# The first feature chunk behind a full-width norm taken as two products in a hybrid decoder trunk

## The reference, cut to what matters

```python
for layer in range(DEPTH):
    h = rms_norm(r, norm_mix_pre[layer])
    proj = h @ w_in[layer]
    ...                                   # two attention branches, gates
    mix = (...) @ w_out[layer]
    r = r + rms_norm(mix, norm_mix_post[layer])
    h = rms_norm(r, norm_ffn_pre[layer])
    gu = h @ w_gate_up[layer]
    ff = (silu(gu[..., :D_FF]) * gu[..., D_FF:]) @ w_down[layer]
    r = r + rms_norm(ff, norm_ffn_post[layer])
```

## Time and profile before

| | us |
|---|---|
| median of 3 runs (lowest to highest) | 797.07 (796.63 to 797.28) |
| the profiled execution's own time | 796.88 |
| its span | 795.1 |
| PE busy (share of the span) | 787.6 (99%) |
| PEld busy | 763.7 (96%) |
| DVE busy | 575.2 (72%) |
| ACT busy | 452.1 (57%) |
| POOL busy | 135.8 (17%) |

### The profile page before, as it was taken

The page is one execution under the profiler, slowest core; times in us unless marked ns, Lnnn a source line. Parts: engine busy times, 40 slices in busy tenths (PEclk is TensorE's granted clock), DMA queues, the critical chain, the costliest instruction groups (busy, mean ns, idle before and its releaser), DMA issues.

```text
span 795.1 us, 16819 instructions
## 1 busy us (share of the span) xinstructions
PE 787.6 (99%) x6300; PEld 763.7 (96%) x6300; DVE 575.2 (72%) x964; ACT 452.1 (57%) x766; POOL 135.8 (17%) x146
## 2 busy tenths in 40 slices
PE   9999999999999999999999999999999999999997
PEld 9999899999999999999999999999999999999885
DVE  6899787686787666766668987976867977676432
ACT  6657665674565444455557467566755754544331
POOL 0212000233421111101122202000433211111000
PEclk9999999999999999999999999999999999999999
DMA  9767333355266555355654674334652766657951
GB/s 335 260 219 240 129 108 105 108 182 162 57 202 216 165 169 174 119 165 169 195 174 134 197 239 149 107 106 133 181 168 77 220 212 183 193 175 197 274 134 53
DMA packets 55531, 134.87 MB, mean 170 GB/s; under 512 B 20896, under 2 KB 21536, under 8 KB 55344
## 3 DMA queue, kind: packets, MB, share of 16 engines
q1 hardware_dynamic: 38608, 131.43, 52.5%
q10 hardware_dynamic: 16864, 2.62, 1.9%
HBM read 131.93 MB, written 2.10 MB: 169 GB/s over the span
## 4 chain that ended last, share of the span: by engine, by line
PE 98%; DMA 0%; DVE 0%; ACT 0%; issue 0%; DVEq 0%
PE bank L1327 25%; PE bank L1329 24%; PE bank L1328 24%; PE bank L1361 4%; PE bank L1748 3%; PE bank L1749 3%; PE bank L1747 3%; PE bank L1352 2%; PE bank L1602 2%; PE bank L1571 2%; PE bank L1621 1%; PE bank L1420 1%; PE bank L1573 1%; PE bank L1377 1%; PE bank L1576 1%; PE bank L1381 1%
## 5 line engine op out<-in xcount | busy, mean ns | idle before, releaser
L880 DVE TENSOR_TENSOR w_lo<-w_raw,w_hi 128x1024 fp32r<-128x1024 f32 x246 | 331.0, 1348 | 37.7 <-ACT w_hi L436 34.3
L1327 PE MATMUL bank<-h_hi,w_hi 128*128 128x272 f32 (+1 forms) x1200 | 346.0, 288 | 0.0
L1329 PE MATMUL bank<-h_hi,w_lo 128*128 128x272 f32 (+1 forms) x1200 | 342.8, 286 | 0.0
L1328 PE MATMUL bank<-h_lo,w_hi 128*128 128x272 f32 (+1 forms) x1200 | 341.9, 285 | 0.0
L436 ACT ACTIVATE w_hi<-w_raw 128x1024 fp32r<-128x1024 f32 x246 | 258.9, 1056 | 121.5 <-PE bank L1329 56.4
L1327 PEld LDWEIGHTS bank<-h_hi,w_hi 128*128 128x128 f32 x1200 | 226.2, 189 | 0.5
L1329 PEld LDWEIGHTS bank<-h_hi,w_lo 128*128 128x128 f32 x1200 | 226.2, 189 | 0.0
L1328 PEld LDWEIGHTS bank<-h_lo,w_hi 128*128 128x128 f32 x1200 | 226.0, 188 | 0.0
L845 POOL TENSOR_TENSOR pbuf<-sbuf,ubuf 128x272 f32<-128x272 f32 (+1 forms) x44 | 38.4, 874 | 205.6 <-DVE ubuf L1257 204.0
L778 POOL TENSOR_TENSOR acc<-acc,sq 128x272 f32<-128x272 f32 (+1 forms) x45 | 47.5, 1055 | 137.0 <-ACT sq L449 136.8
L1257 DVE TENSOR_TENSOR ubuf<-bank,rstd_h 128x272 f32<-128x272 f32 (+1 forms) x44 | 18.9, 431 | 44.8 <-PE bank L1329 44.8
(11 more groups left out here) (238 smaller groups left out, 1234.7 us busy)
## 6 DMA issues: line engine op xcount, KB each, us to landing
w_raw<-weights SPq DMA_DIRECT2D x216, 512.0 KB, 4.0
w_raw<-weights SPq DMA_DIRECT2D x16, 384.0 KB, 3.6
w_raw<-weights SPq DMA_DIRECT2D x16, 320.0 KB, 2.9
w_first<-first_weights SPq DMA_DIRECT2D x2, 512.0 KB, 7.6
x_tok<-x_rows SPq DMA_DIRECT2D x1, 1024.0 KB, 11.3
turn<-y ACTq DMA_DIRECT2D x4, 256.0 KB, 7.2
r_tok<-turn ACTq DMA_DIRECT2D x8, 128.0 KB, 5.6
out_tokens<-o_tok SPq DMA_DIRECT2D x4, 256.0 KB, 2.0
```

What stands on the lines that cost most here:

```text
L880: dve.tensor_tensor(w_lo[:, n % RING, :], w_raw[:, n % RAW, :], w_hi[:, n % RING, :].bitcast(f32), ALU.subtract).then_inc(lo_ready, 1)
L1327: pe.matmul(dst, wh, hi, start=first, stop=False)
L1328: pe.matmul(dst, wh, lo, start=False, stop=False)
L1329: return pe.matmul(dst, wl, hi, start=False, stop=last)
```

## The change

What TensorE needs of chunk 0 is the high and low part of (old residual + normed part) times the gain. Since the product is linear, it is now taken in two: one on the old residual's chunk 0, which is known long before, and one on the normed part alone. Three matmuls per tile on the old residual's parts (`old_hi`, `old_lo`) are issued ahead of and behind the spread, where dummies stood (two tiles each; 8 dummies are left, ahead of `first_tiles`). `first_tiles` then takes the normed part (`new_hi`, `new_lo`) in place of chunk 0. ScalarE makes `old_hi` after squaring tile 5 of the projection, VectorE `old_lo` after copying tile 6. VectorE's add of chunk 0 to the residual moves from the head of `residual` behind the fourth chunk's add, since the full chunk 0 is still needed (`hh[0]`, `hl[0]`, by later tiles, and its square). Chunks are made in the order 1, 2, 3, 4, 0, 5, 6, 7.

```diff
+CHUNK_ORDER = [1, 2, 3, 4, 0, 5, 6, 7]
...
+        (old_hi, old_lo, new_hi, new_lo, new), _end = place(att0 + 4 * 2 * FC * TOK, [
+            ("old_hi", [P, TOK], f32r), ("old_lo", [P, TOK], f32r), ("new_hi", [P, TOK], f32r), ("new_lo", [P, TOK], f32r), ("new", [P, TOK], f32)])
...
 # ScalarE
+            def old_high(b):
+                t0 = boundary_from(b)
+                act.activation(old_hi[:, t0:], r[:, 0, t0:], ACT.Copy, scale=first_gain(b)).then_inc(old_hi_ready, 1)
...
             def boundary(b, K, g, l):
-                for c in range(KC):
-                    act.wait_ge(r_ready, KC * (b - 1) + c + 1)
+                def high(c):
                     act.activation(hh[:, c, t0:], r[:, c, t0:], ACT.Copy, scale=gain[:, l, g + c:g + c + 1]).then_inc(h_hi, 1)
-                    square(K, c, r[:, c, t0:], t0)
+                act.wait_ge(new_ready, b)
+                act.activation(new_hi[:, t0:], new[:, t0:], ACT.Copy, scale=first_gain(b)).then_inc(new_hi_ready, 1)
+                for c in CHUNK_ORDER:
+                    if c == 0:
+                        act.wait_ge(r_first_ready, b)
+                    else:
+                        act.wait_ge(r_ready, (KC - 1) * (b - 1) + c)
+                    high(c)
+                    square(K, CHUNK_ORDER.index(c), r[:, c, t0:], t0)
...
                     square_tile(K0 + POST_MIX, TL("out") + m, m)
+                    if m == 5:
+                        old_high(2 * l + 1)
 # VectorE
+                dve.scalar_tensor_tensor(out=new[:, t0:], in0=y[:, 0, t0:], scalar=gain[:, lp, gp:gp + 1],
+                                         in1=ps[7][:, 64 + t0:64 + TOK], op0=ALU.mult, op1=ALU.mult).then_inc(new_ready, 1)
...
-                product(0)
-                add(0)
                 product(1)
                 add(1)
-                for c in range(2, KC):
+                product(2)
+                new_low()
+                add(2)
+                for c in range(3, KC):
                     product(c)
                     lo_part(b, c - 2, *nxt(b), t0)
                     add(c)
+                    if c == 4:
+                        dve.wait_ge(new_ready, b)
+                        dve.tensor_tensor(r[:, 0, t0:], r[:, 0, t0:], new[:, t0:], ALU.add).then_inc(r_first_ready, 1)
+                    if c == 6:
+                        lo_part(b, 0, *nxt(b), t0)
...
                     to_y(K0 + POST_MIX, TL("out") + m, m)
+                    if m == 6:
+                        old_low(2 * l + 1)
 # TensorE
+            def old_part(b, tiles):
+                pe.wait_ge(old_lo_ready, b)
+                slot_ready(tiles[-1][1])
+                for t, n, _, t0 in tiles:
+                    bank_free(t)
+                    dst = ps[bank_of(t)][:, t0:TOK]
+                    pe.matmul(dst, w_hi[:, n % RING, 0:P], old_hi[:, t0:], start=True, stop=False)
+                    pe.matmul(dst, w_lo[:, n % RING, 0:P], old_hi[:, t0:], start=False, stop=False)
+                    pe.matmul(dst, w_hi[:, n % RING, 0:P], old_lo[:, t0:], start=False, stop=False)
...
-            def post_norm(K):
+            def post_norm(K, b, tiles):
                 norm_sums(K, 7, t0)
-                keep_clock(10)
+                old_part(b, tiles[:2])
                 norm_spread(K, 7, t0)
-                keep_clock(28)
+                old_part(b, tiles[2:])
+                keep_clock(8)
```

More of the change, by code:

```diff
@@ L900, in lo_part @@
             def lo_part(b, c, g, l, t0):
-                dve.wait_ge(h_hi, KC * b + c + 1)
+                dve.wait_ge(h_hi, made_before(b, c) + 1)
                 dve.scalar_tensor_tensor(out=hl[:, c, t0:], in0=r[:, c, t0:], scalar=gain[:, l, g + c:g + c + 1],
@@ L1338, in tile, with first_tiles, part, part_ready @@
                 mm.then_inc(pe_done, 1)
-            def first_tiles(tiles, ready):
-                if tiles[0][1]:
+            def old_part(b, tiles):
[7 more added lines that the diff above has]
+                    pe.matmul(dst, w_hi[:, n % RING, 0:P], old_lo[:, t0:], start=False, stop=False)
+            def first_tiles(tiles, ready, b=0):
+                if not b:
                     slot_ready(tiles[-1][1])
-                bank_free(max((t for t, *_ in tiles), key=lambda t: -1 if plan.before[t] is None else plan.before[t]))
+                    bank_free(max((t for t, *_ in tiles), key=lambda t: -1 if plan.before[t] is None else plan.before[t]))
                 hi_sem, lo_sem, base = ready
+                def part(q, k, src, t0):
+                    if b and k == 0:
+                        return (new_hi, new_lo)[q][:, t0:]
+                    return src[k][q]
+                def part_ready(q, k):
+                    if b and k == 0:
+                        pe.wait_ge((new_hi_ready, new_lo_ready)[q], b)
+                    else:
+                        pe.wait_ge((hi_sem, lo_sem)[q], (made_before(b, k) if b else base + k) + 1)
                 def low(k):
-                    pe.wait_ge(lo_sem, base + k + 1)
+                    part_ready(1, k)
                     for t, n, src, t0 in tiles:
-                        mm = pe.matmul(ps[bank_of(t)][:, t0:TOK], w_hi[:, n % RING, k * P:(k + 1) * P], src[k][1],
+                        mm = pe.matmul(ps[bank_of(t)][:, t0:TOK], w_hi[:, n % RING, k * P:(k + 1) * P], part(1, k, src, t0),
                                        start=False, stop=k == KC - 1)
@@ L1357, in first_tiles @@
                 for k in range(KC):
-                    pe.wait_ge(hi_sem, base + k + 1)
+                    part_ready(0, k)
                     for t, n, src, t0 in tiles:
                         for q, w in enumerate((w_hi, w_lo)):
-                            pe.matmul(ps[bank_of(t)][:, t0:TOK], w[:, n % RING, k * P:(k + 1) * P], src[k][0],
-                                      start=k == 0 and q == 0, stop=False)
+                            pe.matmul(ps[bank_of(t)][:, t0:TOK], w[:, n % RING, k * P:(k + 1) * P], part(0, k, src, t0),
+                                      start=not b and k == 0 and q == 0, stop=False)
                     if k:
@@ L1457, in norm_spread, with h_from, latent_tiles @@
                 spread(K, bank, t0)
+            def h_from(a):
+                return [(hh[:, k, a:], hl[:, k, a:]) for k in range(KC)]
+            def latent_tiles(l):
+                start = [T0(l) if q < QC else 0 for q in range(BANKS)]
+                return [(plan.tile[l, "lat", q], plan.slot[l, "lat", q], h_from(a), a) for q, a in enumerate(start)]
             pe.wait_ge(warm_ready, 1)
@@ L1464, in _ @@
                 TL = lambda name, i=0: plan.tile[l, name, i]
-                full = [(hh[:, k, :], hl[:, k, :]) for k in range(KC)]
-                late = [(hh[:, k, t0:], hl[:, k, t0:]) for k in range(KC)]
+                full, late = h_from(0), h_from(t0)
                 if l == 0:
@@ L1471, in _ @@
                 else:
-                    first_tiles([(TL("lat") + q, S("lat") + q, *((late, t0) if q < QC else (full, 0))) for q in range(BANKS)],
-                                (h_hi, h_lo, KC * 2 * l))
+                    first_tiles(latent_tiles(l), (h_hi, h_lo, KC * 2 * l), 2 * l)
                 slot_ready(S("lat") + 4)
@@ L1709, in _ @@
                     tile(TL("out") + m, S("out") + m, 0, P, late, t0)
-                post_norm(K0 + POST_MIX)
                 g0, gt = S("gu"), TL("gu")
-                first_tiles([(gt + q, g0 + q, late, t0) for q in range(BANKS)], (h_hi, h_lo, KC * (2 * l + 1)))
+                tiles = [(gt + q, g0 + q, late, t0) for q in range(BANKS)]
+                post_norm(K0 + POST_MIX, 2 * l + 1, tiles)
+                first_tiles(tiles, (h_hi, h_lo, KC * (2 * l + 1)), 2 * l + 1)
                 for j in range(4, 4 + RING):
```

31 lines of the change are left out of this document (26 added, 5 removed).

## The result

The changed kernel takes 798.94 us (median of 12 runs, 798.62 to 799.36) against 797.00 (12 runs, 796.46 to 797.48): ratio 1.0026, 95% interval 1.0018 to 1.0034. It is slower by 1.9 us; I had forecast 795.8, and the time lies outside my range.

The account below looks back on a forecast made before the run. TensorE was taken to bound the kernel, so only its start at three boundaries could move: 1.41 us won less 0.17 lost gives 1.24 us off, 795.8 us against the median. Range 795.2 to 797.0 us.

Parts of the forecast that it names:

- What bounds the kernel: TensorE holds 98% of the chain of waits; at boundary 1, 4.42 us pass before the next product's first matmul.
- the add leaves the chain: At each boundary's start ScalarE takes `new` directly, without waiting for VectorE's add: 0.47 us each, 1.41 us in all.
- What is put ahead of the spread: Six old-part products replace ten dummies ahead of the spread, ending it later by 0.09, 0.03 and 0.05 us: 0.17 lost.
- The parts made early: `old_hi` and `old_lo`, made during the projection's last tiles, cost nothing; GpSimd's last add still ends just in time.
- The start as a whole: TensorE starts the first tiles earlier by 0.38, 0.44 and 0.42 us at the three boundaries: 1.24 us.
- the hand-over of 0.14 us: Time from the end of ScalarE's high part to the first matmul, taken from the old profile.
- Whether the start's lead survives: In the first tiles VectorE's extra low part delays chunk 7's add about 0.40 us; 0.76 us of lead stay.
- the point of decision: TensorE's wait at chunk 7 decides once VectorE's add comes more than 0.76 us later than forecast.
- rival 2: VectorE's stream becomes the bound at chunk 7: 0.5 us per boundary, 798.5 us; milder: GpSimd's adds stretch its instructions; chance 0.06.
- Rival 1: Six old products ahead of the spread run slower, 0.4 us per boundary: 796.9 to 797.1 us; chance 0.12.
- Rival 3: Spread loses nothing, start gains the full 0.47 us each, measurement falls low: 795.7 to 795.2 us; chance 0.14.
- The rule on the pipe: Trainium skill: VectorE's next instruction waits until the previous one's pipe has emptied; by it, 798.5 us.

Follow-up runs that it names:

- experiment 5: Changed kernel with chunk 0's add early and its parts last, minus 8 dummies: 795.71 us; kernel before with bank and slot waits ahead of the 28 dummies: 796.90 us.
- experiment 1: GpSimd's adds of squares at the three boundaries replaced by constant writes: on the changed kernel 795.29 us, on the kernel before 796.90 us.

## Why the prediction was wrong

**What bounds the kernel; the add leaves the chain.** Right. ScalarE's `new_hi` starts 0.03 us after VectorE's `new` ends.

**What is put ahead of the spread.** Right. From sums to `new` it is 2.70 us where it was 2.62: 0.08 lost, 0.09 forecast; the spread starts 0.13 later after the sums, 0.14 forecast. At boundaries 2 and 3 the loss is 0.04 and 0.05 us, 0.03 and 0.05 forecast.

**The parts made early.** Right, but only just. GpSimd's last add ahead of the sums lasts 1.46 us at boundary 1 and 1.26 at boundary 3 and ends 0.21 and 0.09 us before them; the sums follow the projection's last product by 0.13 and 0.12 us, as before.

**The start as a whole.** Mis-sized: 1.53 us measured, 1.24 forecast. The term that failed is the hand-over of 0.14 us to the first product, which I carried over to a product with one wait; it is 0.05, and three times 0.09 is the difference (experiment 5).

**Whether the start's lead survives.** This is the step that failed, and it turned the sign. It said that VectorE has one low part more ahead of chunk 7's add, "about 0.40 us of its pace", so that the add comes 9.46 us behind the first product's row at 205.69, with 0.76 us in hand. It comes 11.09 us behind `new` (205.28 to 216.37), 1.63 later than that and so 0.87 beyond the point of decision. The durations 0.43, 0.48 and 0.61 were read off a stream in which GpSimd's add always lay under the PSUM product, and I took them for properties of the instructions. They belonged to the phase: experiment 1 changes only what GpSimd does, and the add falls from 1.00 to 0.42 us. Nor was chunk 7 the only tight one; chunk 5 was late too, which I had not looked at.

**The rivals.** I gave "slower by over 0.2%" 0.07. The case that came is rival 2 in its milder form, GpSimd's adds stretching VectorE's instructions, to which I gave 0.06 together with its main form; that its 798.5 us came within 0.5 of the time is luck, since the price was worked out for its main form, an engine without overlap. Rival 1 is refuted by the spread's rows. Rival 3's larger gain at the start is real, though it came from the hand-over and not from a spread without loss, and more than twice as much (3.59 us against 1.53) was lost behind it. The rule on the pipe that I had weighed plays no part: VectorE's instructions still start 0.35 us after an add that lasts 0.43.

**What stays open.** Why a boundary loses 0.48 in one case and 0.93 in another follows from where each GpSimd add falls, which I read from the traces but did not compute beforehand. The start of boundary 1 differs by up to 1.1 us between kernels whose code ahead of it is nearly the same (202.50 to 203.64); I did not pursue it. What happens when GpSimd's adds leave the boundary altogether, for example to ScalarE, was not tried.

## What to carry to other kernels

Before you insert an instruction into a stream that runs beside GpSimd, lay the other engine's rows under it: a duration read from a trace holds only for the phase in which it was read. If both engines read SBUF, and VectorE's instruction has two tensors there, put it where GpSimd has nothing to do (ahead of its first add or behind its last), and move what feeds GpSimd along with it; one without the other came out level with the kernel before (+0.1 and +0.5 us), both together turned +1.9 us into -1.5, and -1.1 when run again. And count the waits that stand at the instruction on the critical path: those that are met long before can stand earlier.

## What the runs showed of the hardware

- VectorE's add of two SBUF tensors (128x272, fp32) lasts 0.43 us alone, 0.44 inside a GpSimd write of 0.75 us, and 1.00 us when it starts 0.06 to 0.25 us into a GpSimd add. A product with its second tensor in PSUM lasts 0.48 beside the same GpSimd add.
- It goes both ways: GpSimd's add takes 0.97 us when it starts 0.09 us behind a VectorE add, 0.85 when 0.22 behind, and 0.77 when a PSUM product is under way.
- Inside GpSimd's add the held VectorE instruction ends 0.28 to 0.31 us behind it, wherever in the add it started (0.06 to 0.67 us in).
- The first matmul of 272 columns that had to wait for one other engine is followed by the next after 0.23 us, not 0.125: such a wait costs TensorE 0.10 us beyond its length. Behind the several waits of the kernel before it is 0.20.
- A matmul that stands behind several waits, all but one met long ago, starts 0.14 to 0.15 us after the last is met; with one wait it takes 0.05 to 0.06.
